# Two blocks in fp32 with dense experts for most tokens: gathering the chosen experts' rows for 48 tokens in place of 32

## The reference, cut to what matters

```python
def peer_ffn(h, w_query, sub_keys, expert_u, expert_v):
    q = (hc @ w_query).reshape(chunk, PEER_HEADS, PEER_QDIM)
    s1 = jnp.einsum('thd,nd->thn', q[..., :half], k1)
    s2 = jnp.einsum('thd,nd->thn', q[..., half:], k2)
    v1, i1 = lax.top_k(s1, PEER_TOPK)
    v2, i2 = lax.top_k(s2, PEER_TOPK)
    ...
    sc, pos = lax.top_k(cand, PEER_TOPK)
    eidx = jnp.take_along_axis(cidx, pos, axis=-1)
    g = jax.nn.softmax(sc, axis=-1)
    u = jnp.take(expert_u, eidx, axis=0)
    a = jnp.einsum('thkd,td->thk', u, hc)
    act = jax.nn.gelu(a, approximate=False) * g
    vv = jnp.take(expert_v, eidx, axis=0)
    return jnp.einsum('thk,thkd->td', act, vv)
```

## Time and profile before

| | |
|---|---|
| median of three runs | 1343.72 us |
| the profiled execution, its own time | 1346.77 us |
| its span, first to last instruction | 1344.6 us |
| granted TensorE clock, mean | 0.994 |
| PE, DVE, ACT, POOL busy | 98%, 75%, 61%, 37% |
| stretch of U slots 0 to 47 | about 298 to 427 us |
| of U slots 48 to 127 with the gates | 427 to 681 us |
| of V | 681 to 1012.5 us |

### The profile page before, as it was taken

How to read it: one execution, slowest core, us unless ns; L and a number is a source line. 1 busy time by engine, 2 the same in 40 slices (tenths; PEclk the granted TensorE clock), 3 DMA queues, 4 the chain that set the end, 5 groups by cost and what they waited for, 6 DMA issues and landing times.

```text
span 1344.6 us, 24822 instructions
## 1 busy us (share of the span) xinstructions
PE 1314.7 (98%) x9818; PEld 1259.7 (94%) x9818; DVE 1010.1 (75%) x1849; ACT 823.8 (61%) x1679; POOL 503.8 (37%) x248
## 2 busy tenths in 40 slices
PE   9999899999999999999999999999998999999997
PEld 9998799999999999999989899999998999999997
DVE  4573545859999888899878788998858846888843
ACT  6563656545455888888755555555556666665553
POOL 4745466678801000000034344333102453763442
PEclk9999999999999999999999999999999999999999
DMA  8433345556556555455579999998763544555552
GB/s 304 142 110 111 113 138 175 172 162 187 192 199 216 173 164 172 163 167 164 167 267 326 338 332 321 338 330 318 271 209 117 168 142 141 174 160 177 179 190 95
DMA packets 74299, 268.36 MB, mean 200 GB/s; under 512 B 8252, under 2 KB 8636, under 8 KB 74184
## 3 DMA queue, kind: packets, MB, share of 16 engines
q1 hardware_dynamic: 64968, 233.22, 53.1%
q0 software_dynamic: 9216, 33.56, 6.8%
HBM read 265.70 MB, written 1.05 MB: 198 GB/s over the span
## 4 chain that ended last, share of the span: by engine, by line
PE 81%; DVE 12%; ACT 4%; DMA 1%; issue 1%; POOL 0%; SPq 0%; DVEq 0%; ACTq 0%
PE PS L600 80%; DVE SPL L1515 2%; ACT SPL L1077 2%; DMA RAW<-in_ev 1%; DVE ixu L1805 1%; DVE Ssc L1799 1%; DVE ixu L1796 1%; DVE bias L1594 0%; DVE top L1802 0%; DVE top L1793 0%; DMA RAW<-in_dense 0%; DVE HF L1532 0%; DVE qpc L1845 0%; DVE abu L1861 0%; PE PS L743 0%
## 5 line engine op out<-in xcount | busy, mean ns | idle before, releaser
L1077 ACT ACTIVATE SPL<-RAW 128x1024 fp32r<-128x1024 f32 x432 | 455.8, 1057 | 356.4 <-PE PS L600 342.9
L600 PE MATMUL PS<-HS,SPL 128*128 128x224 f32 (+2 forms) x4016 | 542.7, 293 | 6.9 <-DVE SPL L1515 4.0
L600 PEld LDWEIGHTS PS<-HS,SPL 128*128 128x128 f32 x4016 | 511.0, 190 | 21.1 <-DVE SPL L1515 7.2
L2237 POOL TENSOR_TENSOR SPL<-RAW,SPL 128x1024 fp32r<-128x1024 f32 x148 | 360.1, 2437 | 347.9 <-ACT SPL L1077 347.7
L1515 DVE TENSOR_TENSOR SPL<-RAW,SPL 128x1024 fp32r<-128x1024 f32 x284 | 354.4, 1250 | 164.0 <-ACT SPL L1077 162.3
L600 PE MATMUL PS<-asp,SPL 128*128 128x448 f32 (+1 forms) x2048 | 326.9, 322 | 3.0 <-DVE SPL L1515 1.8
L600 PEld LDWEIGHTS PS<-asp,SPL 128*128 128x128 f32 x2048 | 307.9, 190 | 21.6 <-DVE SPL L1515 2.1
L2267 POOL DMA_INDIRECT rows<-in_er,RS x16 | 26.9, 1681 | 282.1 <-PE PS L600 250.1
L600 PE MATMUL PS<-HXb,SPL 128*128 128x256 f32 x720 | 88.6, 282 | 2.4 <-DVE SPL L1515 1.7
L600 PEld LDWEIGHTS PS<-HXb,SPL 128*128 128x128 f32 x720 | 85.8, 188 | 3.9 <-DVE SPL L1515 2.8
L1290 ACT ACTIVATE oh<-oh,T3f 128x128 f32<-128x128 f32 x224 | 71.4, 404 | 0.0
(11 more groups left out here) (286 smaller groups left out, 1459.6 us busy)
## 6 DMA issues: line engine op xcount, KB each, us to landing
RAW<-in_dense SPq DMA_DIRECT2D x176, 512.0 KB, 3.5
RAW<-in_eu SPq DMA_DIRECT2D x128, 512.0 KB, 3.5
RAW<-in_ev SPq DMA_DIRECT2D x128, 512.0 KB, 5.2
bias<-in_nab SPq DMA_DIRECT2D x2, 768.0 KB, 8.2
XT<-in_xT SPq DMA_DIRECT2D x4, 256.0 KB, 5.8
out_y<-HF SPq DMA_DIRECT2D x4, 256.0 KB, 2.2
c<-in_c SPq DMA_DIRECT2D x1, 960.0 KB, 10.3
c<-in_c SPq DMA_DIRECT2D x1, 512.0 KB, 4.7
```

The source lines that it names most:

```text
L600: return e.matmul(out, l, r, start=start, stop=stop, skip_group_check=skip)
L1077: e.activation(spl(n)[0], raw(n), ACT.Copy).then_inc(*up("act_high", ("hi", n)))
L2237: e.tensor_tensor(lo, raw(n), hi.bitcast(f32), ALU.subtract).then_inc(*up("pool_low", ("lo", n)))
```

## The change

- 16 more tokens (TB) are gathered, so W is 208: tokens 208 to 223. Their rows go through one buffer each for u and v; their work lies in U. In U slot e = 57, 61, ... 117 (`early_slots`) VectorE multiplies the u rows by `xrowb`, and two slots later it adds up the v rows in `yrowb`. GpSimd issues the u gather at slot e - 3 and the v gather at e - 1. The first gather of the other 32 moves from U slot 60 to 121.
- Low parts of the odd slots among U 53 to 119 (34 of them) are made by GpSimd.
- PE: 8 more calls of `mm` for `xrowb` (U slots 12 and 13), 8 of 32 x 32 in U slot 49, which bring the row numbers and gates of the new tokens in place, and 8 in the last V slot, which fold `yrowb`. 52 gate steps in place of 56, spread over the same 76 slots.
- `marks` reads the row of numbers 0 to 127 from PSUM, where ScalarE copies it once, and not from SBUF.
- The parts of the activations in V are made for two slots at once, before each even slot; before, one slot before every slot. `asp` begins 16 bytes further on.
- The extra loads of V (`LATE`) come with slot 27 instead of 25. `ssum` moves to another tile.

```diff
-W = T - TG
+TB = 16
+W = T - TG - TB
...
     if EXPERT + LISTED <= n < AFTER + 4:
-        return True
+        return not (ROUTED + 5 <= n - EXPERT < ROUTED + 72 and (n - EXPERT) % 2 == 1)
...
     ahead = 0
     while u < NE:
-        if u >= NE - 4:
+        if u in (NE - 4, NE - 2):
             yield "a", ahead
-            ahead += 1
+            ahead += 2
         yield "u", u
         u += 1
     for j in range(NE):
-        while ahead < min(j + 4, NE):
+        if j % 2 == 0 and ahead < min(j + 4, NE):
             yield "a", ahead
-            ahead += 1
+            ahead += 2
...
+def early_slots():
+
+    return {ROUTED + 9 + 4 * j: j for j in range(TB)}
...
-        asp = [top_.take(f"asp{i}", 512, f32r) for i in range(4)]
+        asp_ = top_.take("asp", 2064, f32r)
+        asp = [asp_[:, 4 + 512 * i:516 + 512 * i] for i in range(4)]
...
-        LATE = 25
+        LATE = 27
...
+        marks_iota = bank(7)[:, 0:128]
...
-                    if i in (8, 9):
-                        ps = take("scr", "xrow", i - 8)
+                    if i in (8, 9, 12, 13):
+                        name, k = ("xrow", i - 8) if i < 12 else ("xrowb", i - 12)
+                        ps = take("scr", name, k)
...
+                    if i == ROUTED + 1:
+                        rowsb = take("g", "rowsb")[:, 0:2 * TB].rearrange("p (b n) -> p b n", b=2)
+                        w.wait_ge(*at("picks"))
+                        for g in range(8):
+                            q = slice(32 * (g // 2), 32 * (g // 2) + 32)
+                            t = mm(rowsb[q], con("rowb")[:, 16 - 16 * (g % 2):48 - 16 * (g % 2)],
+                                   picks[:, :, TB * g:TB * g + TB], g % 2 == 0, g % 2 == 1)
...
+                        w.wait_ge(*at("yrowb", TB - 1))
+                        for c in range(8):
+                            mm(bank(VB[c])[:, W:W + TB], yrowb[:, c * 128:c * 128 + 128], con("foldb"), False, False, True)
...
                 elif what == "a":
                     w.wait_ge(*at("gated4", W // 4 - 1))
-                    w.wait_ge(*at("ev", "u", i))
+                    w.wait_ge(*at("ev", "u", i + 1))
                     if i >= 4:
-                        w.wait_ge(*at("v", i - 4))
-                    e.activation(asp[i % 4][:, 0:W], GB[:, i, :], ACT.Copy).then_inc(*up("act_part", ("ahi", i)))
+                        w.wait_ge(*at("v", i - 3))
+                    e.activation(asp2(i)[:, :, 0, 0:W], GB[:, i:i + 2, :], ACT.Copy).then_inc(*up("act_part", ("ahi", i)))
...
                 elif what == "u":
                     split(cur[0] + NSPL)
                     cur[0] += 1
+                    if i in early:
+                        j = early[i]
+                        w.wait_ge(*at("urowb", j))
+                        w.wait_ge(*at("ev", "xrowb", 1))
+                        e.scalar_tensor_tensor(urow[0], urow[0], 1.0, xrowb, ALU.mult, ALU.mult,
+                                               accum_out=hrowb[:, j:j + 1]).then_inc(*up("dve_row", ("dotb", j)))
+                    if i - 2 in early:
+                        j = early[i - 2]
+                        w.wait_ge(*at("vrowb", j))
+                        w.wait_ge(*at("hrowb", j))
+                        if j == 0:
+                            t = e.tensor_scalar(yrowb, vrow[0], hrowb[:, 0:1], None, ALU.mult)
+                        else:
+                            w.wait_ge(*at("yrowb", j - 1))
+                            t = e.scalar_tensor_tensor(yrowb, vrow[0], hrowb[:, j:j + 1], yrowb, ALU.mult, ALU.add)
+                        t.then_inc(*up("dve_row", ("yrowb", j)))
...
+                if what == "u" and i + 3 in early:
+                    j = early[i + 3]
+                    w.wait_ge(*at(*(("dotb", j - 1) if j else ("rowb",))))
+                    e.indirect_dma_start(urow[0], None, A["er"],
...
+                if what == "u" and i + 1 in early:
+                    j = early[i + 1]
+                    if j:
+                        w.wait_ge(*at("yrowb", j - 1))
+                    e.indirect_dma_start(vrow[0], None, A["ev"].rearrange("a b c -> (a b) c"),
...
-                if (what, i) == ("u", ROUTED + 12):
+                if (what, i) == ("u", ROUTED + 73):
```

More of the change, by code:

```diff
@@ L39 @@
 _at = 0
-for _n, _w in (("ident", 128), ("iota", 128), ("permd", 128), ("permr", 128), ("fold", TG)):
+for _n, _w in (("ident", 128), ("iota", 128), ("permd", 128), ("permr", 128), ("fold", TG), ("foldb", TB),
+               ("rowb", 48)):
     C0[_n] = (_at, _w)
@@ L364, in build @@
         hrow, grow, erow = RS[:, 0:TG], RS[:, TG:2 * TG], RS[:, 2 * TG:3 * TG].bitcast(u32)
+        hrowb, growb, erowb = RS[:, 96:96 + TB], RS[:, 112:112 + TB], RS[:, 128:128 + TB].bitcast(u32)
+        ssum = RS[:, 144:176].rearrange("p (b a h) -> p b a h", b=2, a=2)
         ar = Arena()
         GB = ar.take("GB", NE * W).rearrange("p (i t) -> p i t", t=W)
+        yrowb = ar.take("yrowb", 1024)
+        xrowb = ar.take("xrowb", 1024)
         ar.close()
@@ L1272, in act_program @@
                                      ACT.Copy).then_inc(*up("act_copy", ("ev", "sc", c4, a)))
-            beside = gather_slots()
+            beside, early = gather_slots(), early_slots()
             def gelu(i):
@@ new lines, in act_program @@
+                                     ACT.Copy).then_inc(*up("act_copy", ("copies", "xrow")))
+                    if i == 10:
+                        w.wait_ge(*at("full", "xrow", 1))
+                        e.activation(copies.rearrange("p c (g t) -> p c g t", t=TB),
+                                     HF[:, :, W:W + TB].unsqueeze(2).to_broadcast([128, 8, 128 // TB, TB]),
+                                     ACT.Copy).then_inc(*up("act_copy", ("copies", "xrowb")))
+                    if i in (9, 10, 13, 14):
+                        name, k = ("xrow", i - 9) if i < 13 else ("xrowb", i - 13)
+                        w.wait_ge(*at("full", name, k))
+                        e.activation((xrow if i < 13 else xrowb)[:, 512 * k:512 * k + 512], psum(name, k),
+                                     ACT.Copy).then_inc(*up("act_copy", ("ev", name, k)))
@@ L1966, in angles @@
                     yield
-            routing, turning, beside = route(), angles(), gather_slots()
+            routing, turning, beside, early = route(), angles(), gather_slots(), early_slots()
             for _ in range(4):
@@ L1979, in dve_program @@
                     w.wait_ge(*at("ev", "t3", 1))
-                    w.wait_ge(*at("full", "xrow", 1))
+                    w.wait_ge(*at("full", "xrowb", 1))
                     marks(0)
@@ L2260, in pool_program @@
             run(walk(cur, 16, 8, split, nothing, pair=True))
+            early = early_slots()
             def gather(j):
```

58 lines of the change are left out of this document (43 added, 15 removed).

## The result

The changed kernel takes 1352.22 us, the median of four executions (1351.57 to 1354.36), the kernel before 1344.38 beside it (1343.64 to 1345.4, four). The ratio is 1.0061, 95% interval 1.0047 to 1.0075: slower by 0.6%. The profiled execution took 1351.57 us, its span is 1349.0.

A forecast was written before the change was run, and what follows sets the result against it. PE was taken as the bound, busy 98% of the span. Terms +1.4 - 10.9 + 23.7 + 0.6 - 10.4 gave +4.4 us: span 1349.0, median 1348.1 us, range 1336 to 1356.

The forecast's parts named there:

- What a matmul costs: On PE: a floor of 111 ns; only the large matmul loses 13.3 ns, -0.107 us per slot after U 47.
- every column counts: Rival on PE: no floor, narrower tiles save 0.160 us in all slots; -4.9, 1338.8 us; chance 0.12.
- U slots 0 to 47: First U stage: matmuls gain nothing, `xrowb` calls add 1.8 us, a wait hides 0.4: +1.4 us.
- PE's own work in U 48 to 127: Gated U slots: matmuls -8.6, four fewer gate steps -3.5, slot 49's calls +1.2: together -10.9 us.
- The term of +1.2 for slot 49's 16 small passes: U slot 49 on PE: 8 calls, 16 passes of 32 x 32, at most 1.8 us, at least 0.6, taken +1.2.
- DVE's chain: Gated U slots: rows delay `gated_u` by 1.14 us at 32 odd steps, PE stalls +23.7 us; ungated last slots +0.6.
- GpSimd: Gated U slots: its 2.4 us low parts and gathers cost nothing, and no collision with DVE is added.
- V: V stage: matmuls -13.7, folding `yrowb` +1.8, late weights +1.5: together -10.4 us.
- rival 3: V becomes bound by DMA, 2.54 us a slot, and gains nothing: +11 more, 1359 us; chance 0.10.
- the late weights: V stage: less time to spare and fuller DMA queues make PE wait longer: +1.5 us, bounds 0 and +11.
- 1: Rival on PE: every column counts, so narrower matmuls save more; -4.9, 1338.8 us; chance 0.12.
- 2: Rival in gated U: DVE's order does no harm, -19.3, 1324.4 us; milder, half the stalls, 1336; together 0.17.

The follow-up runs named there:

- rows_last: Changed kernel with the two rows instructions of a U step moved behind `gated_u` in the same step: 1336.13 us, ratio to before 0.9944.
- marks_sbuf: Changed kernel with the marks reading their second operand from SBUF again instead of PSUM: 1365.89 us, ratio to before 1.0172.
- rows_last_spread: Changed kernel with the rows instructions behind `gated_u` and the late loads of V issued apart: 1326.43 us, ratio to before 0.9878.
- narrow_alone: Changed kernel with 208 dense tokens, the 16 tokens' expert part left out and all U low parts on DVE: 1325.48 us, ratio to before 0.9862.
- rows_even: Changed kernel with the rows instructions moved to even steps, where GpSimd makes the low part: 1352.55 us, ratio to before 1.0069.
- rows_last_low_dve: Changed kernel with the rows instructions behind `gated_u` and every low part of U on DVE: 1344.3 us, ratio to before 1.0005.
- spread: Changed kernel with three of V's four extra loads issued later and apart instead of all four together: 1348.73 us, ratio to before 1.003.

## Why the prediction was right

The forecast was a span of 1349.0 and a median of 1348.1 us, slower. The span came out as forecast, to 0.1 us, which is luck: the three stages sum to +5.4 (1.3 + 14.4 - 10.3) and not to +4.4, and the profiled execution of the changed kernel had 1.4 us less ahead of U and 0.4 more behind V. The median is 4.1 us above the number, inside the range; from median to median the change cost 7.8 us. Most of that is the step from the profiled execution to the median: before, the profiled one was 3 us over the median, and I carried that over; in the changed kernel it is the lowest of its four executions, 0.65 us under their median. So a profiled execution isn't always the longer one, and the forecast of the median should have allowed for the scatter of the one execution that it started from. That "slower" came out doesn't hang on this; its size does. By its own steps:

- **What a matmul costs.** A floor of 111 ns, and 13 ns off the large one. Right in U: pitches of 208-column passes are 112 ns in the mean, as those of 224 columns; the pair went from 316 to 303 ns; the new 16-column passes for `yrowb` take 112:

```profile
1008.02 1.94 PE L618 MATMUL PS<-CC,rows 128*128 128x32 f32 x16 [0.31 <-DVE SPL L1561]
1009.80 1.94 PE L618 MATMUL PS<-CC,yrowb 128*128 128x16 f32 x16
1011.59 1.64 PE L618 MATMUL PS<-asp,SPL 128*128 128x416 f32 x9
```

The prediction lets the formula N / 2.4 + 2.5 of the Trainium skill speak for "every column counts". The page "TensorE: Matmul & The Clock Gate", section "Back-to-back issue gap", gives it for an isolated matmul, and says itself that it under-counts small ones in a stream of weight loads and matmuls. The 111 ns of 32 columns bear that out, so the page is no support for that rival.

- **U slots 0 to 47:** +1.4 forecast, 132.3 to 133.6 measured. The wait at slot 29 didn't close, though: it is 0.18 us, so about as much was hidden as forecast.
- **PE's own work in U 48 to 127:** -10.9 forecast, -10.4 measured (the stage's +14.4 less the stalls below). The term of +1.2 for slot 49's 16 small passes was mis-sized. They take 0.28 us, 18 ns each, below my bound of 0.6, so the slots and gate steps gave 1.4 us less than their -12.1, and the two errors nearly cancel. The 0.28 is from the start of the row to that of the next:

```profile
432.79 0.35 PE L618 MATMUL PS<-eqs,CC 128*32 128x32 f32 x16
433.07 1.16 PE L618 MATMUL PS<-oh 128*128 128x128 f32 x8
```

- **DVE's chain:** +24.3 with the last slots. Counted from the starts of the matmuls, drain included, all that a pitch at a wait exceeds the normal one is 3.3 us before and 28.1 after: +24.8. The 21 steps with one gate are the 21 that wait, 0.8 to 1.0 us in all but the first two; the 11 with two gates lose 0.1 to 0.3. A single step of the chain is shown above: +4.38 where 4.2 to 4.4 was forecast. This is the term that carries the forecast, and rows_last shows its cause.
- **GpSimd:** no cost, right; its 34 low parts take 2377 to 2410 ns, and the rows' products show no wait for their gathers' landing. The marks, the other DVE instruction of 1024 elements beside those low parts, don't occur in the prediction's argument that nothing collides; only their input in PSUM kept them out of it, as marks_sbuf shows at 13.7 us.
- **V:** -10.4 forecast, 331.5 to 321.2 measured. The sizes inside are less sure: rival 3 was not the case, but the late weights cost more than the +1.5. PE's one large wait grew from 1.81 us to 4.43, the half clock beside it from 3.4 us to 6.8 (1.7 and some 2.3 us of PE's time), and ScalarE waited 27.7 us for weights in 20 places, 10.7 in 6 before. That makes about +3.2 where +1.5 was forecast. The total fits by luck, because the matmuls gave more. Without its one wait and half clock (1.8 + 1.7) V would last 328.0 us before; rows_last_spread's V, with next to no such loss, lasts 313.9. That is -14.1, where -13.7 + 1.8 = -11.9 was forecast: the matmuls' term was 2 us too small. Why a pair gave more in V than in U wasn't tested.

Of the rivals, 1 is refuted by narrow_alone, and 2 by the waits themselves. Its number of 1324.4 us (a span of 1325.3) isn't reached by taking the stalls away: rows_last, which takes most of them away, has 1336.13 us and a span of 1329.9. Only rows_last_spread, without the late weights in V as well, comes there with 1326.43 and 1322.6. Rival 3 fell too: V is 10.3 us shorter.

## What to carry to other kernels

Before adding work to an engine that isn't full, look for its instruction that releases a buffer of the bound engine, and put the new work behind it: here 1.2 us ahead of it cost 1 us of PE in 21 of 32 steps and 0.1 to 0.3 in the others, and behind it next to nothing, at the same total. Then look at what the new work runs beside: in rows_even it lost as much to GpSimd's low parts as it had lost to the order. Narrowing a matmul whose pitch is on the floor gives nothing (132.3 us with 224 and with 208 columns); look for the shapes above the floor. Loads that only the end of a kernel needs are better issued singly between the weights of a stage whose DMA is nearly full than in one pile: that was worth 3.4 us of V here, and 7.2 with the rows behind `gated_u`.

## What the runs showed of the hardware

- A DVE instruction with both inputs in SBUF and GpSimd's low part hold each other up: 2.73 us instead of 1.22 beside a low part of 2.4, with its end 1.1 us after that of the low part in all nine cases of rows_even, and low parts of up to 3.1 us in marks_sbuf and 3.4 in rows_even. Inputs in SBUF read with zero steps are hit too (the marks). With one input in PSUM both keep their times: 1212 to 1219 and 2377 to 2410 ns.
- The pitch of a pass with 128 x 128 weights is 111 to 112 ns at full clock for 16, 32, 208 and 224 columns alike; with weights of 128 x 32 and 32 columns it is 18 ns. At 32 columns of both kinds it is thus the weights that make the difference.
- PE's long wait in V, 4.3 to 4.8 us, went with 6.8 us at half clock (1.2 GHz) in the changed kernel, narrow_alone, marks_sbuf and rows_last_low_dve, and with 3.4 us in rows_last and rows_even; before, a wait of 1.8 us went with 3.4. The 24 stalls of up to 1.3 us in the changed kernel had none. But in spread the clock was at half for 3.4 us from 1009.0, and PE's longest idle time in the 140 us before was 0.28 us. So the length of the wait alone doesn't tell.
